# A causal convolution beside attention: eight phases instead of four, full-width products instead of three split ones, finished earlier

## The reference

```python
a = a_val * sigmoid(a_gate)                                   # 1040 tokens x 512 channels
a = silu(layer_norm(causal_depthwise_conv(a, conv_w, conv_b), ln_g, ln_b))   # width 31, norm over the 512 channels
o = sparse_index_attention(q, k, v, qi, ki, wi, topk)         # 8 heads of 64, the 256 best keys of each query
m = concatenate([a, o]) @ w_out
```

## Time and profile before

| | |
|---|---|
| median of 3 runs | 2596.41 us (2596.08 to 2597.38) |
| span of the profiled execution, first to last instruction | 2589.3 us |
| what the runs have around that span | 7.1 us |
| PE busy | 2419.0 us (93%) |
| DVE busy | 2029.7 us (78%) |
| ACT busy | 1698.5 us (66%) |
| POOL busy | 696.4 us (27%) |
| TensorE clock granted, mean | 0.968 of full |

### The profile page before, as it was taken

One profiled execution on the slowest core, in us unless ns is written; L12 is line 12 of the kernel. 1 busy time (PEld: TensorE's weight loads), 2 busy tenths in 40 slices (PEclk: granted clock), 3 DMA queues, 4 the chain that ended last, 5 costly groups with the idle time before them and its releaser, 6 DMA issues. The chain is left out here.

```text
span 2589.3 us, 37639 instructions
## 1 busy us (share of the span) xinstructions
PE 2419.0 (93%) x12697; PEld 2079.4 (80%) x12697; DVE 2029.7 (78%) x2587; ACT 1698.5 (66%) x1815; POOL 696.4 (27%) x495
## 2 busy tenths in 40 slices
PE   8989999987979999999999599998979999999997
PEld 8969978875867888888888499996867888888785
DVE  3788876678888899999998543537779998998886
ACT  3369836766217888888877465663147878877775
POOL 0105817762002222222222412120013222222223
PEclk9999999998988999999999699999979999999998
DMA  5502344324339699989898511104359699999994
GB/s 173 141 4 95 82 101 124 89 67 127 108 129 376 228 354 365 367 338 331 297 373 301 189 53 38 41 33 149 98 199 354 238 352 368 375 371 363 377 369 184
DMA packets 114989, 564.74 MB, mean 218 GB/s; under 512 B 23351, under 2 KB 27703, under 8 KB 65616
## 3 DMA queue, kind: packets, MB, share of 16 engines
q1 hardware_dynamic: 89776, 512.19, 54.0%
q0 software_dynamic: 25120, 51.36, 7.2%
HBM read 574.25 MB, written 73.29 MB: 250 GB/s over the span
## 5 line engine op out<-in xcount | busy, mean ns | idle before, releaser
L2213 DVE TENSOR_TENSOR e0wlo<-e0raw,e0whi 128x2048 fp32r<-128x2048 f32 x214 | 486.9, 2289 | 59.3 <-ACT e0whi L2061 59.2
L2061 ACT ACTIVATE e0whi<-e0raw 128x2048 fp32r<-128x2048 f32 x214 | 409.9, 1916 | 91.4 <-PE e0banks L93 78.6
L2213 DVE TENSOR_TENSOR e1wlo<-e1raw,e1whi 128x2048 fp32r<-128x2048 f32 x138 | 313.0, 2287 | 43.2 <-ACT e1whi L2061 43.1
L2061 ACT ACTIVATE e1whi<-e1raw 128x2048 fp32r<-128x2048 f32 x138 | 264.0, 1914 | 39.9 <-PE e1banks L93 34.2
L91 PE MATMUL e0banks<-e0whi,e0xh 128*128 128x512 f32 x576 | 231.6, 402 | 1.1 <-DVE e0xl L2218 1.0
L93 PE MATMUL e0banks<-e0whi,e0xl 128*128 128x512 f32 x576 | 226.2, 393 | 0.0
L92 PE MATMUL e0banks<-e0wlo,e0xh 128*128 128x512 f32 x576 | 225.3, 391 | 0.0
L2213 DVE TENSOR_TENSOR e_wu<-e1raw,e_wu 128x2048 fp32r<-128x2048 f32 x70 | 160.2, 2291 | 17.0 <-ACT e_wu L2061 17.0
L91 PE MATMUL odd_banks<-h2T_hi,odd_w_hi 128*128 128x348 f32 x480 | 171.6, 357 | 0.8 <-DVE h2T_lo L2533 0.5
L2061 ACT ACTIVATE e_wu<-e1raw 128x2048 fp32r<-128x2048 f32 x70 | 134.3, 1919 | 49.0 <-PE e1banks L93 30.8
L92 PE MATMUL odd_banks<-h2T_lo,odd_w_hi 128*128 128x348 f32 x480 | 155.0, 323 | 0.0
(11 more groups left out here) (523 smaller groups left out, 7052.6 us busy)
## 6 DMA issues: line engine op xcount, KB each, us to landing
e0raw<-in_moe_w_gate SPq DMA_DIRECT2D x72, 1024.0 KB
e0raw<-in_moe_w_up SPq DMA_DIRECT2D x72, 1024.0 KB
e0raw<-in_moe_w_down SPq DMA_DIRECT2D x72, 1024.0 KB
e1raw<-in_moe_w_gate SPq DMA_DIRECT2D x70, 1024.0 KB
e1raw<-in_moe_w_up SPq DMA_DIRECT2D x70, 1024.0 KB
e1raw<-in_moe_w_down SPq DMA_DIRECT2D x70, 1024.0 KB
qki_w_raw<-in_w_even SPq DMA_DIRECT2D x22, 512.0 KB, 5.7
odd_w_raw<-in_w_odd SPq DMA_DIRECT2D x20, 512.0 KB, 3.8
```

The costliest lines, as they stand in the source:

```text
L2061: act.activation(w_hi[i], raw[:, i, :], ACT.Copy).then_inc(hi_done[i], 1)
L2213: dve.tensor_tensor(w_lo[i], raw[:, i, :], w_hi[i].bitcast(F32), ALU.subtract).then_inc(lo_done[i], 1)
```

## The change

- PH = 8: 128 partitions now hold 8 phases of 16 channels. A row has NPH = 130 columns, there are CG = 32 groups, and SHIFTS = 5 bands for each.
- The taps take `b_raw` and `glu4` as they are, in full float32. The splits `highs` and `lows` are gone. A group is 5 products of 130 columns, and there are 160 in all.
- `glu` has room for four zero columns ahead of each group (PAD), set to zero by POOL in `project_v`. The two DRAM arrays of the layout keep their total size; the load into phases and the store out of them are 8 transfers each, to and from 16 partitions, in place of 4 of 32.
- Three groups come ahead of the first scores, in three banks of PSUM. Then one group of five stands in each of the rounds 0 to 28, ahead of the transposes, or behind the first two transposed groups where the step has three. ACT takes the group's result at the end of the same round.
- CONV_STEPS is 29, so the means start at round 30, centring at 35, variances at 37, root at 42, scaling at 44. Tanh is at round 60 and the last product at 61, fixed.
- `BAND_RING` is 3. SP's order of loads of bands and heads, and POOL's order (w_out is split ahead of the last head), are new. w_out's split tiles have a home of their own.
- `last_step` in `rotary_pairs`, one DVE instruction before, is five in the new layout, since a third of the columns no longer begins at a whole eight.

```diff
-PH = 4
-NPH, TPH = T // PH, TP // PH
+PH = 8
+NPH = T // PH
+PAD = SHIFTS - 1
...
+def phase_runs(a, b):
+    first, last = min(-(-a // PH) * PH, b), b // PH * PH
+    return [(i, j) for i, j in ((a, first), (first, last), (last, b)) if j > i]
...
             for r in range(PH):
-                sp.dma_start(glu[GC * r:GC * (r + 1), :].rearrange("p (g n) -> p g n", g=CG),
+                sp.dma_start(glu[GC * r:GC * (r + 1), :].rearrange("p (g n) -> p g n", g=CG)[:, :, PAD:],
                              glu_d.rearrange("(g c) r n -> c g r n", c=GC)[:, :, r, :]).then_inc(glu_in, 16)
...
-BANDS, BAND_RING = SHIFTS * 3, 2
-FIRST_TAPS, TAPS_A, TAPS_B = 2 * BANDS, 5, 4
-TAPS = CG * BANDS
-CONV_STEPS = -(-(TAPS - FIRST_TAPS) // (TAPS_A + TAPS_B))
+BAND_RING, RAW_AT = 3, 2 * TP
+FIRST_GROUPS = 3
+GROUP_ROUNDS = list(range(CG - FIRST_GROUPS))
+GROUP_IN = {n: g for g, n in enumerate(GROUP_ROUNDS, FIRST_GROUPS)}
+CONV_STEPS = GROUP_ROUNDS[-1] + 1
-MEAN_AT, CENTRE_AT, VAR_AT, ROOT_AT, SCALE_AT, SWISH_AT, OUT_AT = (CONV_STEPS + n for n in (1, 6, 8, 13, 15, 17, 18))
+MEAN_AT, CENTRE_AT, VAR_AT, ROOT_AT, SCALE_AT = (CONV_STEPS + n for n in (1, 6, 8, 13, 15))
+SWISH_AT, OUT_AT = 60, 61
...
+            def taps(g):
+                s = g % BAND_RING
+                pe.wait_ge(band_loaded[s], 16 * (g // BAND_RING + 1))
+                if g >= FIRST_GROUPS:
+                    pe.wait_ge(conv_done, g)
+                for k in range(SHIFTS):
+                    a = PAD - k
+                    last = pe.matmul(conv_out(g), b_raw[:, s, k * P:(k + 1) * P], glu4[:, g, a:a + NPH], start=k == 0, stop=k == SHIFTS - 1)
+                last.then_inc(conv_mm, 1)
...
             for n in range(N + 3 * DEN_AFTER):
-                m = FIRST_TAPS + n * (TAPS_A + TAPS_B)
+                three = n + 1 < N and len(key_groups(STEPS[n + 1][1])) > EARLY_GROUPS
                 if n + AHEAD < N:
                     scores(n + AHEAD)
-                taps(range(min(m, TAPS), min(m + TAPS_A, TAPS)))
+                if n in GROUP_IN and not three:
+                    taps(GROUP_IN[n])
                 if n + 1 < N:
                     turned(n + 1, True)
-                taps(range(min(m + TAPS_A, TAPS), min(m + TAPS_A + TAPS_B, TAPS)))
+                if n in GROUP_IN and three:
+                    taps(GROUP_IN[n])
```

More of the change, by code:

```diff
@@ L1031, in tile, with group, conv_out @@
         def tile(t):
[L1032 removed]
+            return glu4[:, W4 * t:W4 * (t + 1), PAD:]
+        def group(g):
+            return glu4[:, g, PAD:]
+        def conv_out(g):
+            bank = (c_ps, *o_ps)[g] if g < FIRST_GROUPS else c_ps
+            return bank[:, 0:NPH]
         def key_rows(n):
@@ L1162, in means @@
                 for g in gs:
-                    last = pe.matmul(c_ps[:, 0:NPH], phase, glu4[:, g, 0:NPH], start=g == 0, stop=g == CG - 1)
+                    last = pe.matmul(c_ps[:, 0:NPH], phase, group(g), start=g == 0, stop=g == CG - 1)
                 if g == CG - 1:
@@ L1216, in denominators @@
                 last.then_inc(t_mm, 1)
-            pe.wait_ge(padded, 3)
-            taps(range(FIRST_TAPS))
+            for g in range(FIRST_GROUPS):
+                taps(g)
             for n in range(AHEAD):
@@ L1282, in beside @@
                         g = W4 * t + i
-                        act.activation(spare[:, t % 2, i, :], glu4[:, g, 0:NPH], ACT.Tanh, bias=half[:, CG + g:CG + g + 1],
+                        act.activation(spare[:, t % 2, i, :], group(g), ACT.Tanh, bias=half[:, CG + g:CG + g + 1],
                                        scale=half[:, g:g + 1]).then_inc(turned_on, 1)
@@ L1319, in _ @@
             act.wait_ge(ready, 1)
-            act.wait_ge(padded, 3)
-            for g in range(FIRST_TAPS // BANDS):
+            act.wait_ge(padded, 1)
+            for g in range(FIRST_GROUPS):
                 take_conv(g)
-                highs(g + BAND_RING)
             exps(0)
@@ L2966, in load_first @@
                     load_head(sp, 0)
-                    load_band(sp, 1)
+                    for g in range(1, BAND_RING):
+                        load_band(sp, g)
                 with Ctx(nc) as d:
@@ L3014, in trunk @@
                 oT = c.sb("oT", [P, 4, T])
-                bands = [c.sb("band_" + n, [P, BAND_RING * SHIFTS * P], F32R) for n in ("hi", "lo")]
+                homes = [c.sb("out0_" + n, [P, 2, D], F32R) for n in ("hi", "lo")]
                 ahead = Ahead(c, "m0", [pre[:, k * D:(k + 1) * D] for k in range(RAW)],
-                              [tuple(b[:, k * D:(k + 1) * D] for b in bands) for k in range(2)], 2)
-                attention_and_conv(nc, first, band_loaded, qk_loaded, const, v, score, oT, glu4, cb, lnp, a_d, aT, bands, ahead, A["w_out0"])
+                              [tuple(one[:, k, :] for one in homes) for k in range(2)], 2)
+                attention_and_conv(nc, first, band_loaded, qk_loaded, const, v, score, oT, glu4, cb, lnp, a_d, aT, ahead, A["w_out0"])
             picks = Picks(g)
```

136 lines of the change are left out of this document (47 added, 89 removed).

## The result

The changed kernel takes 2608.9 us (median of 5 runs, 2602.4 to 2612.5) against 2596.3 for the one before on the same chip: a ratio of 1.0047, 95% interval 1.0036 to 1.0057. The forecast was 2598.9 with a range from 2586 to 2606. The profiled execution was the slowest of its five (2612.5, span 2610.7).

A forecast was written before the change was run, and what follows sets the result against it. PE was taken to bound rounds with taps, and the layout's DRAM round trip the stage's end. Last product -9.0, stores +11.1 and last_step +0.4 made +2.5 us: 2598.9 us, range 2586 to 2606.

The forecast's parts named there:

- A group of taps: In rounds with taps, a group costs PE 1.1 to 1.2 us, and a round stays at 3.14 us as before.
- rival 2: In rounds with taps, PE waits for ACT's take_conv at the one bank: 0.3 us a round, +8.7, 2607.6; chance 0.17.
- The start: Ahead of the first score, fewer tap records run, so PE is free at about 391.3: 5.6 us earlier, at least 4.5.
- Thirteen rounds without taps: Taps end 13 rounds earlier; bare rounds take 2.35 for 3.14 us: 10.3 us gained, the moved norm costing no change.
- Tanh and what follows: From round 60 to the stores: tanh begins one round later, +2.35, and 32 half-size instructions add 4.5 us in full.
- rival 3: Bare rounds at 2.30 us (-0.6) and the longer tanh hidden behind DVE (-4.5): 2593.8 us; chance 0.16.
- The stores: At the stage's end, stores from 16 partitions run at half rate, 96 GB/s: 22.3 us for 11.2, +11.1 (0 to +13).
- The loads: At the stage's end, the convolution result's loads back from DRAM are unchanged at 9.1 us.
- `last_step`: At the end of a stage, five instructions for one mean four more starts: +0.4 us, at most +0.8.
- Band 9 behind head 2: On SP's queue, band 9's load lands barely before round 6 asks for it: 0 to 1 us, taken as 0.
- The sum: For the whole kernel: last product -9.0, stores +11.1, last_step +0.4, making +2.5 us; without the stores' term -8.6.
- issued behind 608: Sign at the stage's end: stores expected at about 602; issued before 597 or behind 608, the prediction is wrong.

The follow-up runs named there:

- e2: The changed kernel with ACT taking a convolution group's result first in its round's copies instead of last: 2605.2 us.
- e7: The changed kernel with a group's five products issued as three behind the scores and two behind the first turned weights: 2606.5 us.
- e16: The changed kernel with a group's products split three and two, and ACT taking the result between its two copies of turned weights: 2602.3 us.
- e15: The changed kernel with the norm's steps back in the rounds where the kernel before has them (means from round 43, scaling from 57): 2596.05 us.
- e6: The changed kernel with POOL's split of the first output weights behind the last head's split instead of ahead of it: 2606.5 us.
- e12: The changed kernel with five unread filler products of 130 columns in seven rounds only (30, 35, 39, 44, 48, 53, 57): 2606.8 us.
- e5: The changed kernel with tanh starting in round 54 instead of 60 and its products in 55 instead of 61: 2598.0 us.
- e14: The changed kernel with groups spread over 42 rounds, stores tile by tile, each tile's loads issued behind the next tile's store: 2583.6 us.
- e3: The changed kernel with its 29 groups spread over 42 rounds and the norm's steps 13 rounds later: 2596.9 us.
- e9: The changed kernel with groups spread over 36 rounds, products split three and two, the norm behind them, tanh from round 54: 2596.2 us.

## Why the prediction was wrong

Taken by the steps of the prediction, in its order:

- *A group of taps*: 1.11 us of PE, as said. But "I take 3.14 us a round as before" failed, +6.9 us over 29 rounds. It was rival 2, at 0.17, with 8.7 us for its size, and it measured 0.24 us a round for the 0.3 of that rival. I had named the wait and set it aside, since the group would fill idle time that was there anyway. It didn't fill it: PE is now 90% busy in these rounds (87.74 of 97.83 us), where it was 95%. e2, e7 and e16 show the mechanism, in rounds 2 to 28.
- *The start*, -5.6: -5.5 from the block's opening to the first `biased`, and 0.4 more to round 0. Right. The block itself opened 2.1 us later, which is within the spread of executions.
- *Thirteen rounds without taps*, -10.3: here the forecast failed most, 12.1 us. The bare round at 2.35 was right (31.3 us for 13 in e15 once the clock is taken off, 2.4 each). Wrong was the sentence behind it, that the norm "adds to the rounds it stands in as before, and I count no change". The norm placed right behind the taps costs 6.9 us more than in rounds 43 to 59 (e15), 1.8 of it in its four rounds of means and 0.9 by POOL's split beside DVE's scaling (e6). And the clock falls, which before the change it didn't until round 61: 3.9 us in rounds 37 and 38 of e15. The last 1.3 of the 12.1 stand in e15 as well: 0.5 for bare rounds at 2.4 and 0.8 in rounds 42 to 59, nearly all where the clock fell. In the changed kernel itself the falls took 2.65 us in round 37 (e12) and 2.3 in rounds 55 and 56 (e2). How the other 4.2 of the 6.9 divide is open. I had read PEclk only where it was low before, and didn't ask what less work would do to it.
- *Tanh and what follows*, +6.85: measured +5.7, near, but partly by luck. A tanh costs 0.39 us from start to start, as I had it (eight in 3.19 us). From the first tanh to the store, though, it is 2.4 us more (21.2 for 18.8) where I had put 4.5 on the path in full, as rival 3 doubted; and the first tanh starts 3.3 us later against round 60 than before, for my 2.35.
- *The stores*, +11.1: measured +3.9, the term of the sum that was too large by 7.2. While only the first transfer moves, the rate is 86 to 99 GB/s, the halved rate that I took; but here transfers from different partitions overlapped: the eight of 266 KB land 1.7 us apart (625.9 to 637.8), where one at 96 GB/s needs 2.8, and the mean is 133 GB/s. "Successive transfers from other partitions didn't overlap" was read off, which show means alone and can't tell it. The same window in slices of 0.25 us had a sign of overlap for one us around 618, where the second of the four transfers landed (618.2), while the rest stays near the 190 of the first transfer alone. So four stores from 32 partitions gained next to nothing by overlap, and the step that failed is to carry that over to 16:

```profile
GB/s 191 179 183 187 200 191 196 191 171 187 196 196 191 191 187 187 171 154 204 300 287 262 229 208 200 196 166 183 196 191 200 196 183 183 191 187 187 179 175 29
```

The Trainium skill, "SBUF — State Buffer", section "Door 1: The DMA port swizzle", gives 104 GB/s for the partitions 0 to 15, and the trace comes near it (86 to 99). The same page's "Can I just issue two DMAs to hit both halves?" has two transfers gain 6%; here eight gain about 40% over one, and the measurement decides.

- *The loads*, no change: -1.2. *`last_step`*: five instructions in 2.26 us for one of 1.99, +0.3 for +0.4. *Band 9 behind head 2*: one wait of 1.0 us, the upper end.
- *The sum*: the two misses in the rounds, 6.9 + 12.1 = 19.0 too little, and the one in the stores, 7.2 too much, make 11.8; the rest is -1.0 (opening +1.7, start -0.3, tanh -1.2, loads -1.2), and together that is the 10.8 us between the forecast's +2.5 and the 13.3 measured at SP. Without the oversized term of the stores the forecast would have been further off: that error made up for part of the others. The end of the stage is where the prediction had it, by the round trip and not by attention (6.6 us apart, for my 14).

Of what was to show me wrong, "issued behind 608" did: 621.6. The idle time of PE for ACT ahead of the taps, named there as the sign of rival 2, stands in the trace too (7.8 us in 15 waits).

## What to carry to other kernels

Freed engine time isn't freed path time, and moved work doesn't keep its price: before counting a gain, take the engine's slack in each round that the work leaves and in each that it goes to, round by round of the pattern, and not the mean. Where an engine's idle share grows, look at its granted clock, and compare two kernels round by round before calling an edit a miss: two of mine had won 3.3 and 3.5 us behind a slow start. And where one buffer passes from producer to taker in every round, place both so that neither waits. And check the tail first: a branch that ends behind the others was worth 10 us for two changed numbers (e5).

## What the runs showed of the hardware

- TensorE's clock fell to its lower level (0.50, 1.2 of 2.4 GHz) at 523 in the changed kernel. From 509.5 to the fall PE was busy 10.0 of 13.2 us, and from 516 on 3.9 of 6.7, its longest wait being 2.2 us. Round 37 took 6.00 us with the fall and 3.35 without. The kernel before, at 95% in its rounds 0 to 28 and at 81% in its rounds 42 to 59 (49.28 of 60.64 us), stood at 1.00 from round 1 to 60.
- Stores out of 16 partitions run at 86 to 99 GB/s while one moves and up to 234 in slices of 0.4 us where transfers overlap, 133 in the mean over 16 us; who issues them (one queue or two) makes no difference (16.2 and 16.8 us).
- A DVE pass over 128x1040 with two inputs that starts while POOL is at a subtraction ends 1.1 us behind POOL's pass, however much of that was left: 1.70, 2.04 and 2.37 us in the changed kernel and 3.48 in e14, for 1.24 with POOL idle. When DVE starts first it takes 1.23 and POOL's pass 3.47 instead of 2.40 (e3).
- One program's executions differ by 10 us and more (e14: 2581 to 2592, e9: 2593 to 2609). In e14 the three fast ones have a mean granted clock of 0.970 to 0.971, the two slow ones 0.967 and 0.968; which comes first, the lost time or the lower clock, these means don't tell.
